# Second layer's gate and up products in five groups of seven block products, with the last product's operands split one product ahead and one weight sum made in DRAM

## The chip, the cores and the metric

The kernel runs on one core of a Trainium2 chip. The metric is the device time of one execution in microseconds (us). The engines are the matmul engine (PE, with its weight loads, PEld), VectorE (DVE), ScalarE (ACT), GpSimd (POOL) and SyncE (SP), which mainly issues DMAs.

## The reference

A decoder of two layers over x, 512 tokens by 1024 columns, in float32. Each layer has a mixer (the first a convolution beside differential attention, the second a gated delta rule beside forgetting attention) and then a gated product with D_FF = 2816:

```python
x = x + y @ w_out[l]
h = rms_norm(x, ffn_norm_w[l])
x = x + (jax.nn.silu(h @ w_gate[l]) * (h @ w_up[l])) @ w_down[l]
...
return rms_norm(x, final_norm_w)
```

What is changed is how `h @ w_gate[1]` and `h @ w_up[1]` are computed, and what `@ w_down[1]` needs for that. The mixers are not touched.

## The kernel before

Every operand of a large product is kept as a high part (rounded to the matmul engine's float32r by ACT) and a low part (what is left, by DVE), and a product is three matmuls: high by high, high by low, low by high (`product`, L2170, whose matmuls stand under L2168). "Split" below is that pair of an ACT copy and a DVE subtraction.

**Weights.** Weights come as tiles of 128 x 1024 floats, 512 KB, numbered t in the order of use. SP loads a tile into `raw` (two buffers), ACT and DVE split it into `wring`, a ring of RING = 4 slots, and PE uses it. `hi_ready`, `lo_ready` and `tile_used` are the counters between them: the split of tile t waits until tile t - 4 is used, the load of tile t into raw until the tile that was there is split. Each engine has its own program and does it in order; SP's and POOL's DMAs too go out in the order of their programs.

**First layer, gate and up.** Four plain tiles (`plain_gate_up`) of 8 x 3 = 24 matmuls of 512 columns each make the first two column chunks of gate and of up. The other 20 chunks of each come in GROUPED = 5 groups (`glu_products`, L2484). A group is a product of 512 rows by 1024 by 1024 columns, gate beside up, cut in 2 x 2 blocks and made with seven block products instead of eight: G_M11, G_M12, G_M22, G_M21, G_SUM, G_LAST, G_ALL, each two tiles of 12 matmuls, 14 steps in all. Here the activations are the stationary operand, so a group's result has tokens on the partitions; 16 transposes a group (`turn_results`, L2470, matmuls of L2481) turn it back, and stand in the next group ahead of its steps 4 and 6. The weights of the block products are sums. `x_part`, `y_part` and `w_part` are loaded by SP (`load_part`, L731), POOL's adding DMAs add a second block to x_part or w_part in place (L849), DVE adds y_part to x_part (`sum_weights`), and G_M12's tiles come through raw (L756). `x_part` has two buffers, x_even and x_odd, one for even and one for odd groups. `glu_hi` (L963, copies of L980) and `glu_lo` (L1498, L1504) split the tiles, `glu_results` (L1513) combines the block products on DVE, and `keep_turned` (L1010) copies turned chunks to their place `AF`.

**First layer, down** (`down`, L2503): the last group's transposes stand after the first eight chunk products and wait for DVE's last results.

**Second layer, gate and up** (`gate_up`, L2398): all 44 tiles plain, in a loop over four tiles; DVE evacuates them (L1464), ACT applies silu (L1065), and `ffn_last` on DVE (L1607) makes the chunks and the sums that the last product needs of them (`others`, `pfull`; L1622 to L1636). Before that loop DVE transposes x in blocks of 32 to `turned` (L2129), and SP moves those blocks to `resid`, x with tokens on partitions, with 16 DMAs of 128 KB in pieces of 128 bytes (`residual_blocks`, L774, L782), one after every second tile (RESIDUAL_AFTER, L66).

**Last product** (`w_down[1]`): again 2 x 2 blocks and seven products, of six pieces of up to 12 + 12 matmuls each (`piece`, L2808), in the order of L72: P_12, P_11, P_22, P_21, P_SUM, P_ALL, P_LAST. The blocks of w_down come from `last_d`: B12 through raw, B11 to `kept`, B22 to `more`, and POOL adds to both in place (`add_to_kept`, L896, L907); B11 + B21 + B22 is made by DVE's sums of kept and more (L1688). The left sides are split to their places (L1114, L1692) one product ahead from the third on, `last_lo` (L1643, L1648) splits the weights, and `after_product` (L1654) adds the products to resid.

**What sets the order around the change.** There is no planner here: each engine's program is written out by hand, with counters that say when a buffer is free. PE's order around the change is the second layer's output product (8 tiles), gate and up, the last product, and the end.

```python
            if t >= RESIDUAL_AFTER and (t - RESIDUAL_AFTER) % 2 == 0 and (t - RESIDUAL_AFTER) // 2 < 16:
                residual_blocks((t - RESIDUAL_AFTER) // 2)
...
                elif place is x_part[j % 2] and j >= 2:
                    t = glu_tile(j - 2, G_ALL, p)
                    sp.wait_ge(lo_ready[t % RING], slot_round(t))
```

## Time and profile before

| | |
|---|---|
| Time, median of 3 runs | 1218.61 us (1217.34 to 1218.65) |
| Time of the profiled execution | 1218.75 us |
| Its span, first to last instruction | 1216.9 us |
| PE matmuls busy | 1201.6 us, 99% |
| PE weight loads busy | 972.4 us, 80% |
| DVE busy | 784.4 us, 64% |
| ACT busy | 566.3 us, 47% |
| POOL busy | 107.1 us, 9% |
| Chain that ended last, share of PE | 89% |
| DMA | 138.04 MB, 113 GB/s over the span |

Times in the trace run from the span's start. The profiled execution took 1.85 us more than its span; that lies around the first and last instruction. The share of busy time is an average over stages with different limits, and a busy PE is one that has a matmul under way, not one at its peak: matmuls overlap, so the pace is read from how long many of them take together.

### The profile page before, as it was taken

Reading aid. Unit: us, or ns where it says so; the run is one execution under the profiler, and the core shown is the slowest. Engines: PE = TensorE matmul, PEld = TensorE weight load, DVE = VectorE, ACT = ScalarE, POOL = GpSimd, SP = SyncE. Lnnn points to the kernel's source line nnn. Section 1 sums busy time; section 2 is a strip of 40 time slices with the busy share of each in tenths; the row PEclk is TensorE's granted clock in tenths of the full one; section 3 lists DMA queues with packets and bytes.
Section 4 is the critical chain, followed back from the end, with each engine's and each line's share of the span. In section 5 each row is a group of like instructions: output and inputs, shape, how many; then the busy total and the mean of one; then the engine's idle time right before and its main releaser. Section 6 shows DMA issues by size and latency. Waiting matters only on the chain.

```text
span 1216.9 us, 16112 instructions
## 1 busy us (share of the span) xinstructions
PE 1201.6 (99%) x5831; PEld 972.4 (80%) x5831; DVE 784.4 (64%) x1233; ACT 566.3 (47%) x917; POOL 107.1 (9%) x209
## 2 busy tenths in 40 slices
PE   9999999999999999999999999999999999999998
PEld 7876648888888878888888788788888888888876
DVE  6787886786667763337677666545665455456796
ACT  6354455655555543325585254444243232324564
POOL 0000000011110100000002814400000000000120
PEclk9999999999999999999999999999999999999999
DMA  6243311687867533331322211022244443336881
GB/s 247 90 118 91 106 54 52 225 189 174 210 174 187 108 100 91 100 104 55 119 87 70 87 35 53 18 61 66 83 134 116 116 109 104 93 104 223 167 147 70
DMA packets 56643, 138.04 MB, mean 113 GB/s; under 512 B 21890, under 2 KB 22146, under 8 KB 56322
## 3 DMA queue, kind: packets, MB, share of 16 engines
q1 hardware_dynamic: 48754, 111.44, 28.7%
q0 software_dynamic: 6912, 24.38, 11.4%
q10 hardware_dynamic: 912, 1.35, 0.4%
q8 instruction: 40, 0.66, 0.2%
q14 instruction: 25, 0.20, 0.1%
HBM read 128.61 MB, written 2.10 MB: 107 GB/s over the span
## 4 chain that ended last, share of the span: by engine, by line
PE 89%; DVE 5%; ACT 3%; issue 1%; DMA 1%; ACTq 0%; SPq 0%; DVEq 0%
PE PS L2168 87%; PE PS L2481 1%; DVE wring L1648 1%; DMA raw<-w_stream 1%; PE PS L2244 1%; DVE resid L1652 0%; DVE kept L1688 0%; DVE cacc L1843 0%; ACT wring L924 0%; ACTq L1194 0%; DVE wring L1698 0%; PE PS L2559 0%; DVE AA L1692 0%; DVE out L2159 0%; DVE amax L1761 0%
## 5 line engine op out<-in xcount | busy, mean ns | idle before, releaser
L2168 PE MATMUL PS<-HH,wring 128*128 128x512 f32 x2136 | 506.2, 393 | 0.9 <-DVE vd L2094 0.9
L2168 PEld LDWEIGHTS PS<-HH,wring 128*128 128x128 f32 x2136 | 395.2, 188 | 81.4 <-issue 1.3
L2168 PE MATMUL PS<-wring,HH 128*128 128x512 f32 x672 | 156.0, 390 | 0.3 <-ACT wring L1139 0.3
L2168 PEld LDWEIGHTS PS<-wring,HH 128*128 128x128 f32 x672 | 125.7, 188 | 26.6 <-issue 0.6
L1698 DVE TENSOR_TENSOR wring<-raw,wring 128x1024 fp32r<-128x1024 f32 x91 | 111.8, 1231 | 48.2 <-ACT wring L924 48.1
L924 ACT ACTIVATE wring<-raw 128x1024 fp32r<-128x1024 f32 x91 | 95.8, 1056 | 96.0 <-PE PS L2168 68.6
L2168 PE MATMUL PS<-AS,wring 128*128 128x512 f32 x528 | 120.4, 389 | 0.0
L2168 PEld LDWEIGHTS PS<-AS,wring 128*128 128x128 f32 x528 | 99.0, 188 | 20.5
L2168 PE MATMUL PS<-wring,AA 128*128 128x512 f32 x462 | 105.4, 389 | 1.6 <-DVE wring L1648 0.8
L2168 PEld LDWEIGHTS PS<-wring,AA 128*128 128x128 f32 x462 | 86.6, 188 | 20.3 <-issue 2.3
L1464 DVE TENSOR_TENSOR ubuf<-PS,rstd 128x512 f32<-128x512 f32 x22 | 15.2, 690 | 83.9 <-PE PS L2168 83.9
L2168 PE MATMUL PS<-AA,wring 128*128 128x512 f32 x264 | 63.5, 394 | 0.4 <-DVE AA L1777 0.3
L2168 PEld LDWEIGHTS PS<-AA,wring 128*128 128x128 f32 x264 | 49.0, 188 | 11.7 <-issue 1.0
L952 ACT ACTIVATE wring<-raw 128x1024 fp32r<-128x1024 f32 x44 | 46.1, 1049 | 25.0 <-PE PS L2168 21.0
L1456 DVE TENSOR_TENSOR wring<-raw,wring 128x1024 fp32r<-128x1024 f32 x44 | 53.7, 1219 | 6.3 <-ACT wring L952 6.3
L2168 PE MATMUL PS<-wring,left_minus 128*128 128x512 f32 x240 | 56.8, 393 | 0.0
L1065 ACT ACTIVATE gbuf<-gbuf 128x512 f32<-128x512 f32 x22 | 13.9, 632 | 83.4 <-DVE gbuf L1464 83.4
L2168 PEld LDWEIGHTS PS<-wring,left_minus 128*128 128x128 f32 x240 | 44.5, 188 | 8.9
L1571 DVE TENSOR_TENSOR AS<-AF,AS 128x512 fp32r<-128x512 f32 x20 | 13.8, 689 | 47.6 <-ACT AS L1027 47.6
L907 POOL DMA_DIRECT2D kept<-w_last x12 | 10.4, 869 | 362.3 <-DVE wring L1648 344.3
L1504 DVE TENSOR_TENSOR wring<-x_even,wring 128x1024 fp32r<-128x1024 f32 x24 | 29.4, 1224 | 19.2 <-ACT wring L980 19.1
L849 POOL DMA_DIRECT2D x_even<-w_glu x12 | 10.5, 875 | 325.7 <-DVE wring L1504 325.7
(367 smaller groups left out, 1606.1 us busy)
## 6 DMA issues: line engine op xcount, KB each, us to landing
raw<-w_stream SPq DMA_DIRECT2D x131, 512.0 KB, 3.5
x_even<-w_glu POOLq DMA_DIRECT2D x12, 512.0 KB, 6.3
raw<-w_glu SPq DMA_DIRECT2D x10, 512.0 KB, 9.4
y_part<-w_glu SPq DMA_DIRECT2D x10, 512.0 KB, 6.6
w_part<-w_glu SPq DMA_DIRECT2D x10, 512.0 KB, 5.3
w_part<-w_glu POOLq DMA_DIRECT2D x10, 512.0 KB, 10.9
kept<-w_last POOLq DMA_DIRECT2D x10, 512.0 KB, 8.3
x_odd<-w_glu POOLq DMA_DIRECT2D x8, 512.0 KB, 6.2
```

The costliest lines, as they stand in the source:

```text
L924: nc.scalar.activation(wring[:, t % RING, 0], raw_tile(t), ACT.Copy).then_inc(hi_ready[t % RING], 1)
L952: nc.scalar.activation(wring[:, t % RING, 0], raw[:, t % RAW], ACT.Copy).then_inc(hi_ready[t % RING], 1)
L1065: nc.scalar.activation(gbuf[:, c], gbuf[:, c], ACT.Silu).then_inc(sem("gate_silu"), 1)
L1456: V.tensor_tensor(wring[:, t % RING, 1], raw[:, t % RAW], wring[:, t % RING, 0].bitcast(f32), ALU.subtract).then_inc(lo_ready[t % RING], 1)
L1464: V.tensor_tensor(buf[:, c], PS[:, 2 * c + u], rstd[:], ALU.mult).then_inc(evacuated, 1)
L1504: V.tensor_tensor(wring[:, t % RING, 1], glu_source(j, a, p), wring[:, t % RING, 0].bitcast(f32), ALU.subtract).then_inc(lo_ready[t % RING ...
L1571: V.tensor_tensor(AS[:, k % RING, 1], kept_chunk(k), AS[:, k % RING, 0].bitcast(f32), ALU.subtract).then_inc(sem("ffn_lo"), 1)
L1648: V.tensor_tensor(wring[:, t % RING, 1, 0:n], tile_source(g), wring[:, t % RING, 0, 0:n].bitcast(f32), ALU.subtract).then_inc(lo_ready[t % ...
L1698: V.tensor_tensor(wring[:, t % RING, 1], raw_tile(t), wring[:, t % RING, 0].bitcast(f32), ALU.subtract).then_inc(lo_ready[t % RING], 1)
L2168: return nc.tensor.matmul(out, lhsT, rhs, start=start, stop=stop, skip_group_check=adds)
L2244: last = nc.tensor.transpose(PS[:, bank, blk(j)], src[:, u % 2, blk(j)], ident)
L2481: last = nc.tensor.transpose(PS[:, TURN_BANK + c % 2, blk(b)], glu_result(b)[:, blk(c)], ident)
```

## The change

It does the following.

1. Second layer: four plain tiles, then five groups of seven block products as in the first layer, with the same functions, which now take the layer as their first argument. `gate_up` and DVE's and ACT's `ffn_last` go. After `load_group(1, 0)` SP issues the sixteen `residual_blocks`, all in a row, and then goes on with `load_group(1, 1)`. The blocks are transposed by DVE in steps 4 to 7 of the first group.
2. `x_part` has one buffer for all groups of both layers. It is loaded for group j + 1 as the last thing of `load_group(l, j)`, when G_ALL's tiles of group j are split.
3. First layer, down: half of the next two column products go ahead of each pair of transposes.
4. Last product: the order is P_12, P_11, P_21, P_22, P_SUM, P_LAST, P_ALL, four of the seven go on in a bank that holds an earlier one, the left sides lie in two places for even and odd products (`place_even`, `place_odd`) and are split one product ahead throughout, halves of columns are made during the groups (`halves`), cross sums in `cross`. The last group's transposes stand after three pieces of P_12.
5. B11 + B21 + B22 is made in DRAM (`w_sums`) by twelve DMAs of POOL, each waiting for the one before, that start when eight tiles have been used and stand ahead of the first layer's adding DMAs in POOL's program. SP loads it to kept for P_SUM. DVE's sums of kept and more go.

The core of the diff (the index functions with a layer argument, counters and the data layout of the host are left out):

```diff
-T_GLU = T_GU0 + 4
+PLAIN = 4
 GROUPED = 5
 GLU_PRODUCTS = 7
 GLU_STEPS = 2 * GLU_PRODUCTS
-T_DN0 = T_GLU + GROUPED * GLU_STEPS
+T_DN0 = T_GU0 + PLAIN + GROUPED * GLU_STEPS
 T_IN1 = T_DN0 + KF
 T_OUT1 = T_IN1 + 29
 T_GU1 = T_OUT1 + KD
-T_DN1 = T_GU1 + 2 * KF
+T_DN1 = T_GU1 + PLAIN + GROUPED * GLU_STEPS
+T_GLU = (T_GU0 + PLAIN, T_GU1 + PLAIN)
 AWAY = GROUPED * GLU_STEPS
-N_TILES = T_DN1 - AWAY
+N_TILES = T_GU1 + PLAIN - AWAY
 HALF = KF // 2
...
-P_12, P_11, P_22, P_21, P_SUM, P_ALL, P_LAST = range(PRODUCTS)
-OUT_ORDER = (2, 3, 0, 1)
-BANK_12, BANK_21, BANK_SUM, BANK_22 = 4, 6, 0, 2
-PRODUCT_BANK = (BANK_12, BANK_21, BANK_12, BANK_21, BANK_SUM, BANK_22, BANK_SUM)
+P_12, P_11, P_21, P_22, P_SUM, P_LAST, P_ALL = range(PRODUCTS)
...
+OUT_ORDER = (0, 1, 2, 3)
+PRODUCT_BANK = (4, 0, 4, 0, 2, 0, 4)
+CONTINUED = (P_21, P_22, P_LAST, P_ALL)
+ON_KEPT = (P_11, P_21, P_SUM, P_ALL)
 ADDED = (P_21, P_LAST, P_ALL)
 ADDING = 3
+SUM_PARTS, SUM_STEPS = 4, 3
...
+def uses_raw(t):
+    return not RAW <= t < FIRST and (not away(t) or (t - T_GLU[t >= T_GLU[1]]) % GLU_STEPS // 2 == G_M12) and t < T_DN1 + PIECES
...
-    AA, p = at("AA", [KF, 2, S], f32r, p)
-    gbuf, p = at("gbuf", [2, S], f32, p)
-    ubuf, p = at("ubuf", [2, S], f32, p)
+    AA, _ = at("AA", [KD, 2, S], f32r, p)
...
     AF, q = at("AF", [ENDING, S], f32, at_A)
-    AS, _ = at("AS", [RING, 2, S], f32r, q)
-    x_odd, q = at("x_odd", [2, TILE], f32, q)
+    at_left = q
+    AS, _ = at("AS", [RING, 2, S], f32r, at_left)
     left_diff, q = at("left_diff", [4, 2, 2 * P], f32r, q)
     left_minus, q = at("left_minus", [4, 2, S], f32r, q)
-    x_even, q = at("x_even", [2, TILE], f32, q)
+    at_parts = q
+    x_part, q = at("x_part", [2, TILE], f32, q)
...
     y_part, q = at("y_part", [2, TILE], f32, q)
     w_part, q = at("w_part", [2, TILE], f32, q)
+    pfull, q = at("pfull", [HALF, 2 * P], f32, q)
     assert q <= TOP, (q, TOP)
-    x_part = (x_even, x_odd)
     scaled, q = at("scaled", [KD, S], f32, at_A + 6 * S * 4)
+    turned, _ = at("turned", [NB, KD, P], f32, at_A + 6 * S * 4)
     diff_full, q = at("diff_full", [4, 2 * P], f32, q)
...
+    place_even, q = at("place_even", [HALF, 2, 2 * P], f32r, at_left)
+    assert q <= at_parts
+    place_odd, q = at("place_odd", [HALF, 2, 2 * P], f32r, at_parts)
+    assert q <= at_parts + 6 * TILE * 4
...
-        def load_part(place, sem_at, j, kh, u):
+        def load_part(l, place, sem_at, j, kh, u):
             for p in range(2):
                 n = sem_at + p
-                if place is w_part and j:
-                    t = glu_tile(j - 1, G_LAST, p)
+                if j:
+                    t = glu_tile(l, j - 1, G_LAST if place is w_part else G_M22 if place is y_part else G_ALL, p)
                     sp.wait_ge(lo_ready[t % RING], slot_round(t))
-                elif place is y_part and j:
-                    t = glu_tile(j - 1, G_M22, p)
-                    sp.wait_ge(lo_ready[t % RING], slot_round(t))
-                    sp.wait_ge(sem("lhs_made"), weights_summed(j - 1, p))
-                elif place is x_part[j % 2] and j >= 2:
-                    t = glu_tile(j - 2, G_ALL, p)
-                    sp.wait_ge(lo_ready[t % RING], slot_round(t))
-                sp.wait_ge(part_loaded[n], 16 * (j + 1))
-                sp.dma_start(place[:, p], glu_d[j, kh, u][:, p * TILE:(p + 1) * TILE]).then_inc(part_loaded[n], 16)
+                    if place is y_part:
+                        sp.wait_ge(sem("lhs_made"), weights_summed(l, j - 1, p))
+                sp.wait_ge(part_loaded[n], part_count(l, j) - 16)
+                sp.dma_start(place[:, p], glu_d[l, j, kh, u][:, p * TILE:(p + 1) * TILE]).then_inc(part_loaded[n], 16)
+        def load_group(l, j):
+            if j == 0:
+                load_part(l, x_part, 0, j, 0, 0)
+            for p in range(2):
+                t = glu_tile(l, j, G_M12, p)
+                before = raw_before(t)
+                sp.wait_ge(hi_ready[before % RING], slot_round(before))
+                sp.wait_ge(lo_ready[before % RING], slot_round(before))
+                sp.dma_start(raw[:, t % RAW], glu_d[l, j, 0, 1][:, p * TILE:(p + 1) * TILE]).then_inc(raw_loaded[t % RAW], 16)
+            load_part(l, y_part, 2, j, 1, 1)
+            load_part(l, w_part, 4, j, 1, 0)
+            if j + 1 < GROUPED:
+                load_part(l, x_part, 0, j + 1, 0, 0)
         sp.wait_ge(tile_used, T_OUT0 + RING)
         for j in range(GROUPED):
-            load_part(x_part[j % 2], 0, j, 0, 0)
-            for p in range(2):
-                t = glu_tile(j, G_M12, p)
-                before = t - GLU_STEPS if j else T_GLU - RAW + p
-                sp.wait_ge(hi_ready[before % RING], slot_round(before))
-                sp.wait_ge(lo_ready[before % RING], slot_round(before))
-                sp.dma_start(raw[:, p], glu_d[j, 0, 1][:, p * TILE:(p + 1) * TILE]).then_inc(raw_loaded[p], 16)
-            load_part(y_part, 2, j, 1, 1)
-            load_part(w_part, 4, j, 1, 0)
+            load_group(0, j)
...
                 sp.wait_ge(feed_sq, KD * FINAL)
+                sp.wait_ge(h_ready, KD * FINAL)
+                sp.wait_ge(sem("lhs_scaled"), 2 * KD)
...
-            if t == ROW_AFTER:
-                sp.wait_ge(ssq_done, 7 * FINAL)
-                sp.dma_start(final_w[:].rearrange("p a b -> p (a b)"), final_d).then_inc(small_loaded, 16)
-            if t >= RESIDUAL_AFTER and (t - RESIDUAL_AFTER) % 2 == 0 and (t - RESIDUAL_AFTER) // 2 < 16:
-                residual_blocks((t - RESIDUAL_AFTER) // 2)
+        sp.wait_ge(tile_used, T_GU1)
+        for j in range(GROUPED):
+            load_group(1, j)
+            if j == 0:
+                for m in range(16):
+                    residual_blocks(m)
         for i in range(PIECES):
             t = last_tile(i)
-            sp.wait_ge(hi_ready[(t - RAW) % RING], slot_round(t - RAW))
-            sp.wait_ge(lo_ready[(t - RAW) % RING], slot_round(t - RAW))
+            before = raw_before(t)
+            sp.wait_ge(hi_ready[before % RING], slot_round(before))
+            sp.wait_ge(lo_ready[before % RING], slot_round(before))
             n = len(piece_rows(i)) * S
             sp.dma_start(raw[:, t % RAW, 0:n], last_d[B12][:, columns_of(i)]).then_inc(raw_loaded[t % RAW], 16)
         sp.wait_ge(tile_used, T_DN1)
         for i in range(PIECES):
+            sp.wait_ge(kept_loaded[i], kept_count(P_11) - 16)
             sp.dma_start(kept_tile(i), last_d[B11][:, columns_of(i)]).then_inc(kept_loaded[i], 16)
+        sp.dma_start(more_last[:], last_d[B22][:, 3 * TILE:HALF * S]).then_inc(first_loaded[1], 16)
+        sp.wait_ge(sem("glu_turned"), 8 * GROUPED)
         sp.dma_start(more_first[:], last_d[B22][:, 0:3 * TILE]).then_inc(first_loaded[0], 16)
-        sp.wait_ge(sem("ffn_lo"), SPLITS_0 + HALF)
-        sp.wait_ge(sem("lhs_made"), MADE)
-        sp.dma_start(more_last[:], last_d[B22][:, 3 * TILE:HALF * S]).then_inc(first_loaded[1], 16)
+        sp.wait_ge(sem("ffn_lo"), split_count(P_11, PIECES - 1))
+        sp.wait_ge(sem("halves_made"), 2 * HALF)
+        sp.dma_start(final_w, final_d.rearrange("p (u c) -> p u c", u=2)).then_inc(small_loaded, 16)
+        sp.wait_ge(added[0], GROWN_FIRST)
+        for i in range(PIECES):
+            t = last_tile(P_21 * PIECES + i)
+            sp.wait_ge(lo_ready[t % RING], slot_round(t))
+            sp.dma_start(kept_tile(i), sums_d[:, columns_of(i)]).then_inc(kept_loaded[i], 16)
...
+        quarter = HALF * S // SUM_PARTS
+        pool.wait_ge(tile_used, T_IN0 + 8)
+        for step in range(SUM_STEPS):
+            for n in range(SUM_PARTS):
+                columns = slice(n * quarter, (n + 1) * quarter)
+                if step or n:
+                    pool.wait_ge(added[0], 16 * (SUM_PARTS * step + n))
+                if step:
+                    nc.gpsimd.dma_start(sums_d[:, columns], last_d[(B11, B21, B22)[step]][:, columns], accum_op=ALU.add).then_inc(added[0], 16)
+                else:
+                    nc.gpsimd.dma_start(sums_d[:, columns], last_d[B11][:, columns]).then_inc(added[0], 16)
...
+        def grow_group(l, j):
...
+                                accum_op=ALU.add).then_inc(added[d % ADDING], 16)
+        for a, part, behind in ((P_21, B21, P_11), (P_LAST, B21, P_22), (P_ALL, B12, P_SUM)):
             for i in range(PIECES):
-                add_to_kept(a, i, part, behind)
...
+                if g == 4:
+                    keep_turned(1, GROUPED - 1, 0)
+                    left_high(P_12, 4)
+                    keep_turned(1, GROUPED - 1, 2)
+                    left_high(P_12, 5)
+                    keep_turned(1, GROUPED - 1, 1)
+                    keep_turned(1, GROUPED - 1, 3)
                 if g == 9:
...
+        def halves(r):
+            if r == 0:
+                dve.wait_ge(sem("ffn_mul"), MULS + 2)
+            else:
+                dve.wait_ge(sem("glu_kept"), 4 * GROUPED + (2 * r if r < HALF - 2 else 4 * GROUPED - HALF + 1 + r))
+            first, second = kept_chunk(2 * r), kept_chunk(2 * r + 1)
+            V.tensor_tensor(first[:, 2 * P:S], first[:, 2 * P:S], second[:, 2 * P:S], ALU.subtract).then_inc(sem("halves_made"), 1)
+            dve.wait_ge(sem("halves_made"), 2 * r + 1)
+            V.tensor_tensor(pfull[:, r], first[:, 0:2 * P], first[:, 2 * P:S], ALU.subtract).then_inc(sem("halves_made"), 1)
+        def turn_residual(n):
+            if n == 0:
+                dve.wait_ge(sem("ffn_lo"), SPLITS[1] + 1)
+                dve.wait_ge(sem("ffn_hi"), SPLITS[1] + 1)
+                dve.wait_ge(sem("lhs_made"), SUMS + LEFT_SUMS)
+            V.transpose(turned[:, :, n], xT[:, n].rearrange("p (t c) -> p t c", c=P)).then_inc(sem("resid_turned"), 1)
...
+            elif l and 4 <= step < 8:
+                for n in (2 * step - 8, 2 * step - 7):
+                    turn_residual(n)
...
+        def cross(a, i):
+            dve.wait_ge(sem("halves_made"), 2 * HALF)
+            of = P_22 if a == P_LAST else P_21
+            dve.wait_ge(sem("ffn_lo"), split_count(of, i))
+            start, stop = rows_of(i)
+            V.tensor_tensor(full_left(a, i), full_left(a, i), pfull[:, start:stop], ALU.subtract).then_inc(sem("halves_made"), 1)
...
-                if g // PIECES == P_21:
-                    i = g % PIECES
-                    dve.wait_ge(first_loaded[i // 3], 32)
-                    dve.wait_ge(lo_ready[last_tile(g) % RING], slot_round(last_tile(g)))
-                    V.tensor_tensor(kept_tile(i), kept_tile(i), more_tile(i), ALU.add).then_inc(sem("lhs_made"), 1)
...
+            pe.wait_ge(sem("copied"), COPIED)
+            columns(4, range(RING))
+            pe.wait_ge(sem("ffn_mul"), glu_made(0, end, "gate_first", 1))
+            columns(0, (0, 1))
+            turn_results(0, end, (0, 1), TURN_BANK)
+            columns(0, (2, 3))
+            pe.wait_ge(sem("ffn_mul"), glu_made(0, end, "up_second", 1))
+            columns(2, (0, 1))
+            turn_results(0, end, (2, 3), TURN_BANK)
+            columns(2, (2, 3))
+            pe.wait_ge(sem("glu_kept"), COPIED)
...
-        gate_up(T_GU1, E_GU1, 3)
+        plain_gate_up(1, T_GU1, E_GU1)
+        for j in range(GROUPED):
+            glu_products(1, j)
...
+                if a == P_12 and i == 3:
+                    pe.wait_ge(sem("ffn_mul"), glu_made(1, GROUPED - 1, "up_second", 1))
+                    turn_results(1, GROUPED - 1, (0, 2, 1, 3), LAST_TURN_BANK)
```

## Rows read from the trace of the kernel before

**Rows 1.** The page, busy time of each engine with its share of the span

```profile
PE 1201.6 (99%) x5831; PEld 972.4 (80%) x5831; DVE 784.4 (64%) x1233; ACT 566.3 (47%) x917; POOL 107.1 (9%) x209
```

**Rows 2.** The chain that ended last, in the first layer's groups: start, length, what

```profile
296.42 0.87 PE PS L2481 x8
...
303.64 32.66 PE PS L2168 x144
336.30 0.87 PE PS L2481 x8
...
416.10 0.87 PE PS L2481 x8
```

**Rows 3.** Windows: a first-layer group, then plain second-layer tiles (busy us and count by engine)

```profile
325.00:365.00 40.00, 40.00 (x186) 33.26 (x185) 28.06 (x31) 21.27 (x27) 5.21 (x6) 1.00 0.75 185
...
925.00:968.00 43.00, 43.00 (x192) 35.59 (x191) 21.48 (x30) 14.18 (x16) 0.00 (x0) 1.00 0.39 106
```

**Rows 4.** DVE: transposes for resid; subtractions of half rows, with busy time and mean ns

```profile
L2129 DVE STREAM_TRANSPOSE turned<-xT x8: 668/669/711, 876.6 to 880.8; 128x512 f32<-128x512 f32 x8
...
L1622 DVE TENSOR_TENSOR others<-ubuf 128x256 f32 x11 | 4.6, 418 | 0.0
```

**Rows 5.** Timeline at the seam of two groups of the first layer: start, length, engine

```profile
314.25 3.05 SPq L746 DMA_DIRECT2D x_odd<-w_glu  x2
...
315.72 1.23 DVE L1504 TENSOR_TENSOR wring<-x_odd,wring 128x1024 fp32r<-128x1024 f32 x1 [1.49 <-ACT wring L980]
...
318.44 1.23 DVE L1504 TENSOR_TENSOR wring<-x_even,wring 128x1024 fp32r<-128x1024 f32 x1 [1.49 <-ACT wring L980]
319.96 0.86 POOL L849 DMA_DIRECT2D x_even<-w_glu  x1 [12.86 <-DVE wring L1504]
...
325.18 3.05 SPq L756 DMA_DIRECT2D raw<-w_glu  x2
```

**Rows 6.** DMA issues: count, KB each, median us from issue to landing

```profile
raw<-w_stream SPq DMA_DIRECT2D x131, 512.0 KB, 3.5
...
raw<-w_glu SPq DMA_DIRECT2D x10, 512.0 KB, 9.4
...
kept<-w_last POOLq DMA_DIRECT2D x10, 512.0 KB, 8.3
```

**Rows 7.** The resid copies; SP's DMA queue in 905.7 to 906.1 and in 905.2 to 906.3

```profile
L782 SPq DMA_DIRECT2D resid<-turned x16: 597/597/687, 886.9 to 1044.7; - x16
...
DMA to landing us min/median/max: 3.9/4.7/6.1
...
q1 hardware_dynamic: 529, 0.07, 106.7%
...
q1 hardware_dynamic: 1069, 0.18, 89.0%
```

**Rows 8.** Windows: where the granted clock (the third last number) falls

```profile
780.00:784.00 4.00, 3.15 (x27) 2.13 (x26) 3.00 (x8) 2.32 (x6) 0.00 (x0) 1.00 0.00 0
784.00:788.00 4.00, 4.00 (x24) 4.00 (x23) 1.05 (x3) 0.87 (x2) 0.00 (x0) 0.57 0.00 0
```

**Rows 9.** First layer's end: a window, and PE's first transposes after the last group

```profile
440.00:460.00 20.00, 18.50 (x90) 15.25 (x89) 8.72 (x11) 6.19 (x9) 0.00 (x0) 1.00 0.33 106
...
452.05 0.41 PE L2481 MATMUL PS<-consts,hbuf 128*128 128x128 f32 x2 [1.50 <-DVE glu_s L1542]
```

**Rows 10.** Last product: DVE's weight sums, and the window in which they stand

```profile
L1688 DVE TENSOR_TENSOR kept<-kept,more_first 128x1024 f32<-128x1024 f32 x3 | 3.7, 1226 | 0.3
...
1142.00:1166.00 24.00, 22.45 (x98) 17.97 (x98) 21.83 (x27) 13.87 (x21) 5.16 (x6) 1.00 0.67 110
```

**Rows 11.** Eighth tile's result on DVE; POOL's first adding DMA; landings of w_part's DMAs

```profile
56.34 0.69 DVE L1827 TENSOR_TENSOR ub<-hbuf,sqb 128x512 f32<-128x512 f32 x1 [2.41 <-ACT sqb L1185]
...
241.69 1.01 POOL L849 DMA_DIRECT2D x_even<-w_glu  x1 [240.23 <-DVE wring L1504]
...
DMA to landing us min/median/max: 4.2/9.6/12.2
```

More of the change, by code:

```diff
@@ L2126, in _ @@
         out_proj(3, T_OUT1, E_OUT1)
[L2127 to L2130 removed]
+        ffn_gated(1, T_GU1, E_GU1)
         last_product()
@@ L2910 @@
     out = nc.dram_tensor("out_t", (NB, P, D), f32, kind="ExternalOutput").ap()
-    build(nc, *args, out)
+    sums = nc.dram_tensor("w_sums", (P, HALF * S), f32, kind="Internal").ap()
+    build(nc, sums, *args, out)
     r = run_bass_kernel_spmd(nc, [arrays], core_ids=[0])
```

798 lines of the change are left out of this document (392 added, 406 removed).

## The prediction

> **What bounds the kernel now.** The page comes first: the matmul engine (PE) is busy 1201.6 of 1216.9 us, so only PE's own work, or a wait long enough to stop PE, can move the end [rows 1]. VectorE (DVE), ScalarE (ACT) and the DMA matter by what they make PE wait for. The chain of waits shows what a grouped stage costs: in the first layer the transposes of the groups recur at 296.42, 336.30 and 416.10, so a group lasts 39.88 us, and 144 products take 32.66 us, 0.2268 us each [rows 2]. The windows show both stages packed: the plain second layer has PE busy 43.00 of 43.00 us with DVE at 21.48, a group has PE 40.00 of 40.00 with DVE at 28.06 and ACT at 21.27 [rows 3]. PE has no holes in either, so what a hole costs is new time.
>
> **Second layer's gate and up.** Removed: 40 of 44 plain tiles, each 24 products: 960 x 0.2268 = 217.7 us. Added: five groups of 14 tiles of 12 products, 840 x 0.2268, and 80 transposes, of which the trace has eight in 0.87 us. That is five times the measured group, 5 x 39.88 = 199.4 us [rows 2]. **Saved: 18.3 us.** DVE and ACT work stays covered: on a group's 28.06 us DVE gets four subtractions of half rows (0.42 us each) and in the first group eight transposes of 0.67 us [rows 3, 4]; the first group has no results of a group before it to finish. If that cover were gone each microsecond would count, but 12 us per group are free.
>
> **One x_part instead of two.** Both layers now load the next group's first tiles only once the last sum of this group has been split. In a group that begins at 325.4 (its first transposes, at 336.30, come 48 products later) those splits were DVE's at 313.00 and 315.72, and SP issued the reload of that same buffer at 314.25 and 317; the next group's first split was at 318.44 [rows 2, 5]. Such a load lands in about 4.5 us, so the first split moves to about 321, still 4 us ahead of PE. Loads of raw, y and w follow in one burst of some 3.5 MB; even the slow landing of 9.4 us [rows 6] brings raw at 327, and it is needed split at 330.8. I cost this at nothing; what hides it is the ring of four tiles, and the margin is 2 to 4 us a group, which is the first thing to go if DMA is slower (eight seams, at most 3 us each, 24 us).
>
> **Residual moves past SP's queue.** This is the costly part. Before, one of the sixteen small-block copies into resid was issued every second tile. Now all sixteen stand in SP's program after the load of group 1's x_part and before the load of its raw tiles, which PE needs 5.44 us into the group. With G the start of that group: the last x_part load can go at G - 8.4 (316.95 against 325.4) [rows 5], the sixteen issue for 0.60 us each, 9.6 us, and raw is issued at G + 1.5. They share its DMA queue. One copy's 1024 pieces filled 1.1 us at 89% of all DMA engines, and in its dense middle 529 pieces passed in 0.4 us, so a copy costs the engines between 0.8 (0.4 x 1024 / 529) and 1.1 us [rows 7]. I take 0.85, near the dense middle, since copies in a row overlap their ragged ends: 13.6 us. The first block moves about 2 us after its issue (landing 3.9 at the least, less 1.1 of data and a receipt), at G - 6, so they end at G + 7.6. The two adding DMAs of x_part, issued by POOL at G - 4.4 and G - 1.7, take part of the engines: I add 2 us of a possible 5. Raw's own 512 KB take 1.4 us and a receipt of 0.4, so it lands at G + 11.4; high and low split (1.06 and 1.23 us) put it at G + 13.8. PE stands from G + 5.4: 8.4 us. **The stop cannot be made up**, as PE is the bound. After it the results and splits that queued on DVE and ACT come out one by one before the first transposes; I take 1.6 us. **Together +10 us.** Bounds: if only issue counts, raw lands 3.5 us after G + 1.5 [rows 6] and the cost is 2 us; at 1.1 us a copy, with all 5 us of the adding DMAs and 3 us of catching up, it is 17 us; if copies in a row cost 2 us each, near half their 4.7 us landing, 29 us.
>
> **The clock.** The granted clock falls once in this trace: it is 0.57 in 784 to 788, after PE was busy only 3.15 of the 4 us before [rows 8]. That is a stretch at the lower level (1.2 GHz instead of 2.4) and is worth at most 4 x 0.43 = 1.7 us of PE. A stop of 8 us should bring the same; I let it coincide with the catching up above, whose work needs that time anyway, and keep 1.7 us for the upper end. The Trainium skill (TensorE: Matmul & The Clock Gate, "Why this matters for your kernels") warns that an idle gap between bursts of matmuls sends the clock back to half; by that rule alone I would add the 1.7 us and get 1211.
>
> **First layer's end.** PE stands 1.50 us in 440 to 460, since the transposes at 452.05 wait for DVE's glu_s [rows 9]. The change puts 12 more products (2.7 us) ahead of them: **-1.5 us**.
>
> **Into the last product.** The last group's transposes now stand after three pieces (36 products, 8.2 us) of the last product, against the 7.3 us from start to transpose seen in the first layer: no stop. But pieces 4 and 5 need their left sides from those columns: copies, splits, halves of the columns and two low splits follow in a row, some 4 us after the first transposes end, while PE has one piece, 2.7 us: **+1.3 us** (0 to 3). The other left sides are split one product ahead.
>
> **Last product's weights.** DVE's sums kept + more (1.23 us each, five and a half of them) go [rows 10]; where they stood PE was busy 22.45 of 24 us: **-1.0 us** of the 1.55, as cross sums of 0.7 us come in nearby. P_21 now has one product less of lead for its adding DMAs; issued about 15 us before PE's need, with a landing of 8.3 us [rows 6], they stay hidden.
>
> **Weight sum in DRAM.** Twelve DMAs of 720 KB, each waiting for the one before, from about 56 us (the eighth tile's result) [rows 11]. They stand on POOL's queue ahead of the first adding DMA of the first layer, issued at 241.69. So each may take (241.7 - 56.3) / 12 = 15.4 us. The nearest row, the loads and adding DMAs of w_part of 512 KB each, has landings of 4.2 to 12.2 us under load [rows 11], by size 6 to 17 us; alone, as here, I take 7 to 9: done by 165. Other loads there have slack of several tiles: 0 (to +3 for the copies of the convolution's inputs). The Trainium skill (DMA: Bandwidth & Descriptors, "Anatomy of one DMA") fits 2.0 us plus size at 436 GB/s, an estimate of 3.7 us each and 44 us in all, which does not change the sum; it also calls a write to HBM the slowest to confirm, and no row here shows one of that kind.
>
> **Sum**, against the profiled execution (1218.75 us, its span plus 1.85; 0.14 above the median of 1218.61, which is nothing): 1218.75 - 18.3 - 1.5 + 1.3 - 1.0 + 10.0 = **1209.3 us**.
>
> **Rivals.** (1) The copies hardly delay raw (only the issue counts, or raw overtakes them): 10 becomes 0 to 4, so 1199 to 1203. For it: pieces of 128 bytes pass quickly in the dense middle [rows 7]; against it: nothing follows them closely in this trace, and SP's 9.6 us alone are past the margin. (2) **Slower:** the copies in a row cost the queue 2 us or more each. 16 x 2 ends at G + 26, raw is ready at G + 32, and the stop is 27 us with 2 of catching up: 1228. It decides from a stop of about 22 us, 1.6 us a copy. For it: a single copy takes 4.7 us to land, and a raw load with adding DMAs beside it 9.4 against 3.5 [rows 6, 7]; against it, the 1.1 us of engine time. (3) The DRAM chain is slower than 15.4 us a step: at 18 us it ends 31 us late, of which the first group hides 9: about 1231. No row for such a DMA exists; I hold it for unlikely, at twice the row nearest to it. (4) The single x_part leaves a stop of 1 to 3 us at the seven other seams too: 1216 to 1230 with the copies.
>
> **Chances.** Forecast (stop of 5 to 17 us, 1204 to 1216): 0.55. Rival 1: 0.22. Rival 2: 0.10. Rival 3: 0.04. Rival 4: 0.09, half of it slower. Range 1198 to 1222: it leaves out the far half of rival 2, rival 3 and the ends. A measurement of this kernel tells 0.2%, 2.4 us, from no change: faster (below 1216.2) 0.81, same 0.06, slower 0.13.
>
> **What would show it.** Five groups near 39.9 us in both layers, except the second layer's second, near 49; there the first raw split waits for a DMA from w_glu, with sixteen resid issues in one row of SP before it; PE idle near 8 us, the granted clock perhaps low after it; PE full in 445 to 460; about 1 us idle before the fifth piece of the last product. Wrong if PE is full at that seam, if POOL's first x_part addition comes after 242 us, or if groups of the first layer exceed 40 us.

## The result, and the profile after

The changed kernel takes 1221.16 us (median of 12 runs, 1219.51 to 1224.3) against 1217.74 of the kernel before (12 runs): ratio 1.0027, 95% interval 1.0019 to 1.0034. It is slower by 0.27%, where 1209.3 us, faster, was forecast. The profiled execution is 1221.2 us with a span of 1219.4.

The page of after, against [rows 1]: the busy time of each engine, two rows of the slices (the span in 40 equal parts), and the chain that ended last.

```profile
PE 1186.4 (97%) x5791; PEld 959.2 (79%) x5791; DVE 837.8 (69%) x1273; ACT 619.4 (51%) x992; POOL 141.9 (12%) x251
...
PE   9999999999999999999999999999995899999998
...
PEclk9999999999999999999999999999998899999999
...
PE 85%; DVE 6%; ACT 3%; SPq 2%; issue 2%; DMA 2%; ACTq 0%; DVEq 0%
PE PS L2263 82%; SPq L817 2%; PE PS L2559 1%; DMA first_raw<-w_stream 1%; DVE wring L1571 1%; PE PS L2339 1%; DVE cacc L1939 0%; DMA x_part<-w_glu 0%; ACTq L1275 0%; DVE wring L1794 0%; DMA raw<-w_glu 0%; ACT wring L1036 0%; ACT wring L984 0%; DVE turned L1630 0%; DVE amax L1857 0%
```

PE does 15.2 us less work, and the span is 2.5 us longer: PE now stands for 33 us instead of 15. Two slices of the PE row show it (5 and 8), a dip of PEclk lies over them, and the chain has a link that no page of before had: SPq L817, SP issuing the residual copies. The waits of PE name the stops (us in total, times, longest):

```profile
PE PS L2263 <- DVE glu_s L1603: 17.3, 1, 17.3
PE PS L2263 <- DVE glu_q L1589: 1.6, 1, 1.6
...
PE PS L2263 <- DVE place_even L1674: 1.2, 1, 1.2
```

The large one is one stop, in the second layer's second group. The timelines of SP, ACT, DVE and PE there (start, length, engine, line):

```profile
915.21 2.78 SPq L772 DMA_DIRECT2D x_part<-w_glu  x2
918.16 20.49 SPq L817 DMA_DIRECT2D resid<-turned  x16
938.74 1.11 SPq L783 DMA_DIRECT2D raw<-w_glu  x2
...
943.44 1.06 ACT L1036 ACTIVATE wring<-raw 128x1024 fp32r<-128x1024 f32 x1 [19.87 <-DMA raw<-w_glu]
...
944.52 1.23 DVE L1571 TENSOR_TENSOR wring<-raw,wring 128x1024 fp32r<-128x1024 f32 x1 [18.50 <-ACT wring L1036]
946.70 1.23 DVE L1571 TENSOR_TENSOR wring<-raw,wring 128x1024 fp32r<-128x1024 f32 x1 [0.94 <-ACT wring L1036]
947.84 1.28 DVE L1603 TENSOR_TENSOR glu_s<-PS,glu_s 128x512 f32<-128x512 f32 x2
...
926.08 5.78 PE L2263 MATMUL PS<-wring,left_diff 128*128 128x512 f32 x24
949.18 7.77 PE L2263 MATMUL PS<-wring,HH 128*128 128x512 f32 x24 [17.32 <-DVE glu_s L1603]
```

Followed backwards: PE waits for glu_s, which empties a bank; on DVE glu_s stands behind both low splits of raw; ACT's high split waited 19.87 us for raw to land; and SP issued raw only at 938.74, after sixteen copies that took 20.49 us to issue, 1.28 us each. Raw lands at 943.4, 17.4 us into the group; 11.4 was forecast. The releaser that the wait names is the last link, not the cause. The order on DVE has a part in it all the same: the first raw tile was split at 945.75, but PE ran only at 949.18, since glu_s (L1603) stands behind the second split, although its input, the last product of the group before, had been there since about 926. That is at most 3.4 us of the 17.3, an estimate from these rows; no run moved L1603.

The 24 products after the stop take 7.77 us; in the kernel of 1198.7 us below, where PE had waited 0.32 us before them, the same 24 take 5.74 us. Windows of after (busy us and count by engine, granted clock, DMA share, GB/s):

```profile
936.00:940.00 4.00, 0.00 (x0) 0.00 (x0) 0.00 (x0) 0.00 (x0) 0.00 (x0) 0.56 1.07 178
...
948.00:952.00 4.00, 2.82 (x7) 2.25 (x8) 4.00 (x6) 0.56 (x1) 1.72 (x2) 0.50 0.48 139
952.00:956.00 4.00, 4.00 (x16) 3.22 (x15) 2.63 (x4) 2.15 (x3) 0.00 (x0) 0.80 1.04 193
```

The granted clock falls to its lower level (1.2 GHz instead of 2.4) while PE stands, and is still there when PE starts again: 2.0 us more. In the other runs below with a stop of 6.9 us or more at this place the 24 products take 7.51 to 8.48 us, so 1.8 to 2.7 us more.

### The profile page after: what moved, and what is told of

The parts are those of the page before. It is cut to its first block, busy times and chain, and to the rows that moved or that the text cites. A ratio compares the mean times of both kernels' runs of the same rounds, so it can differ in the third digit from the quotient of the medians.

```text
span 1219.4 us, 15948 instructions
## 1 busy us (share of the span) xinstructions
PE 1186.4 (97%) x5791; PEld 959.2 (79%) x5791; DVE 837.8 (69%) x1273; ACT 619.4 (51%) x992; POOL 141.9 (12%) x251
## 4 chain that ended last, share of the span: by engine, by line
PE 85%; DVE 6%; ACT 3%; SPq 2%; issue 2%; DMA 2%; ACTq 0%; DVEq 0%
PE PS L2263 82%; SPq L817 2%; PE PS L2559 1%; DMA first_raw<-w_stream 1%; DVE wring L1571 1%; PE PS L2339 1%; DVE cacc L1939 0%; DMA x_part<-w_glu 0%; ACTq L1275 0%; DVE wring L1794 0%; DMA raw<-w_glu 0%; ACT wring L1036 0%; ACT wring L984 0%; DVE turned L1630 0%; DVE amax L1857 0%
## 5 line engine op out<-in xcount | busy, mean ns | idle before, releaser
L2263 PE MATMUL PS<-HH,wring 128*128 128x512 f32 x1176 | 288.7, 397 | 0.9 <-DVE vd L2191 0.9
L2263 PE MATMUL PS<-wring,HH 128*128 128x512 f32 x1152 | 268.7, 392 | 17.6 <-DVE glu_s L1603 17.3
L2263 PEld LDWEIGHTS PS<-wring,HH 128*128 128x128 f32 x1152 | 217.2, 189 | 63.4 <-DVE glu_s L1603 17.7
L2263 PEld LDWEIGHTS PS<-HH,wring 128*128 128x128 f32 x1176 | 215.0, 188 | 44.0 <-issue 1.3
L1571 DVE TENSOR_TENSOR wring<-x_part,wring 128x1024 fp32r<-128x1024 f32 x80 | 97.9, 1224 | 77.3 <-ACT wring L1036 77.2
L1794 DVE TENSOR_TENSOR wring<-raw,wring 128x1024 fp32r<-128x1024 f32 x91 | 111.9, 1232 | 46.2 <-ACT wring L984 46.2
L1036 ACT ACTIVATE wring<-x_part 128x1024 fp32r<-128x1024 f32 x80 | 84.6, 1060 | 107.1 <-PE PS L2263 45.9
L2263 PE MATMUL PS<-wring,left_minus 128*128 128x512 f32 x480 | 113.8, 393 | 1.6 <-DVE glu_q L1589 1.6
L2263 PEld LDWEIGHTS PS<-AS,wring 128*128 128x128 f32 x528 | 99.0, 188 | 20.5
L2263 PE MATMUL PS<-wring,place_even 128*128 128x512 f32 x264 | 61.1, 390 | 1.2 <-DVE place_even L1674 1.2
L2263 PE MATMUL PS<-wring,left_diff 128*128 128x512 f32 x240 | 56.5, 391 | 0.4 <-DVE hbuf L1600 0.4
```

The source lines that it names most:

```text
L1036: nc.scalar.activation(wring[:, t % RING, 0], glu_source(t, a, p), ACT.Copy).then_inc(hi_ready[t % RING], 1)
L1571: V.tensor_tensor(wring[:, t % RING, 1], glu_source(t, a, p), wring[:, t % RING, 0].bitcast(f32), ALU.subtract).then_inc(lo_ready[t % RING ...
L1794: V.tensor_tensor(wring[:, t % RING, 1], raw_tile(t), wring[:, t % RING, 0].bitcast(f32), ALU.subtract).then_inc(lo_ready[t % RING], 1)
L2263: return nc.tensor.matmul(out, lhsT, rhs, start=start, stop=stop, skip_group_check=adds)
```

## The experiments

Ratios are against runs of the kernel before on the same chip, whose medians were 1217.6 to 1217.7 us; after itself was not run again there. A seam is the change from one group to the next. The recorded expectations count the kernels: the first is the one with the copies behind the loads, the fourth adds the spread transposes to it, the fifth adds the copies in two parts to the fourth, the ninth is the one of 1198.7 us. An edit shifts the line numbers behind it by one to three, so go by the names of the tiles.

**The copies behind the loads.** The copies leave their place ahead of raw and stand behind the w load of the same group.

```
             load_part(l, w_part, 4, j, 1, 0)
+            if l and j == 1:
+                for m in range(0, 16):
+                    residual_blocks(m)
...
-            if j == 0:
-                for m in range(16):
-                    residual_blocks(m)
```

> The kernel after, with one move in SP's program: the sixteen residual copies stand behind the raw, y and w loads of the second layer's second group instead of ahead of them. Nothing is left out. Theory (the copies hold up the raw loads behind them in SP's queue, and this alone made the kernel slower): the PE stop of 17.3 us at 931.9 goes, and so does the half clock behind it, worth 2.3 us: 1221.2 - 19.6 = 1201.6 us, 1200 to 1204. Rival A (the stop is the seam's own: one x_part buffer, y and w loads in one burst, DVE behind): the stop stays or moves to another load, 1215 to 1221. Rival B (the copies take the DMA engines from whatever comes next, the additions to x_part and w_part or the next x_part load): a new stop of 3 to 8 us in that group, 1205 to 1210.

Measured: 1204.1 us (1202.8 to 1205.9), ratio 0.989 (0.988 to 0.991), 17.1 us less than after. The stop at the second product is gone and the clock stays at 1.00. Timeline of SP and of PE at the next seam, 40 us on:

```profile
922.08 35.56 SPq L820 DMA_DIRECT2D resid<-turned  x16
957.73 1.11 SPq L772 DMA_DIRECT2D x_part<-w_glu  x2
...
967.31 5.73 PE L2263 MATMUL PS<-wring,left_diff 128*128 128x512 f32 x24 [2.13 <-DVE hbuf L1600]
```

The theory holds, 2.5 us short of its figure. Rival B's stop in that group did not come, a smaller one did at the next seam: the copies, now behind the y and w loads and beside six of POOL's additions, take 35.56 us of SP, the next x_part load goes late, and PE stands 2.1 us there.

**How the stop grows.** The same move with eight, and with four, of the copies left ahead of raw (`range(8)` or `range(4)` ahead, the rest behind w).

> The kernel after, with eight of the sixteen residual copies ahead of the raw loads as now and the other eight behind the w load. Nothing is left out. It gives the slope of the stop per copy. In the trace of after SP took 20.5 us for sixteen (1.28 us each); in 935 to 940, where the copies had the DMA engines to themselves, 7092 packets of them passed, 0.72 us for a copy's 1024. Theory: the copies cost engine time, and the additions to x_part share it; raw lands 8 x 1.28 = 10 us earlier and the stop is about 7 us: 1211 us, 1208 to 1213. Rival 1 (0.72 us a copy, the rest is the additions and stays): stop of 11.5 us, 1215. Rival 2 (the price is a step, not a slope: a queue that fills up after the first few): either no stop at all, 1202, or nearly all of it, 1219.

> The kernel after, with four of the sixteen residual copies ahead of the raw loads and twelve behind the w load. Nothing is left out. With 16, 8 and 0 ahead PE stood 17.3, 9.6 and 0 us. Theory (a slope of 0.96 us per copy beyond what the margin hides): stop of 5 to 6 us; 1204.1 + 5.5 = 1209.6 us, or 1212 if so short a stop also brings the half clock of 2.3 us that both longer ones brought. Rival (the first copies pass before the additions begin and inside the margin): stop of 0 to 3 us, 1204 to 1207, the clock unbroken.

Measured: 1213.5 us with eight (8 runs; ratio 0.996, 0.995 to 0.997), 1211.6 with four (2 runs; 0.995, 0.993 to 0.997). SP and PE with eight, then with four:

```profile
916.81 13.87 SPq L820 DMA_DIRECT2D resid<-turned  x8
...
940.79 7.88 PE L2266 MATMUL PS<-wring,HH 128*128 128x512 f32 x24 [9.63 <-DVE glu_s L1606]
```

```profile
916.58 4.97 SPq L820 DMA_DIRECT2D resid<-turned  x4
...
937.29 7.80 PE L2266 MATMUL PS<-wring,HH 128*128 128x512 f32 x24 [6.88 <-DVE glu_s L1606]
```

With 0, 4, 8 and 16 copies ahead PE stands 0, 6.9, 9.6 and 17.3 us: 1.7 us a copy for the first four, 0.7 for the next four, 1.0 for the last eight. It is no step, but no straight line either: with eight copies the stop lies between the theory's 7 us and rival 1's 11.5, and the time is above the theory's range; with four both stop and time are near what was expected. The 7.80 us behind a stop of 6.9 us show that this stop brought the lower clock too (with four copies the time is 7.5 us above the kernel with none ahead); stops of up to 2.3 us at the seams left it at 1.00.

**What made a copy dear.** First the same bytes in long rows; then the small pieces with POOL's two additions held back.

```
-            sp.dma_start(to[:, :, a], from_[:, :, b]).then_inc(sem("resid_loaded"), 16)
+            to = resid.rearrange("p t u c -> p (t u c)")[32 * b:32 * b + 32, 1024 * a:1024 * (a + 1)]
+            from_ = turned.rearrange("p t n c -> p (t n c)")[32 * a:32 * a + 32, 1024 * b:1024 * (b + 1)]
+            sp.dma_start(to, from_).then_inc(sem("resid_loaded"), 16)
```

> The kernel after, with sixteen copies of the same 128 KB at the same place in SP's program, but each moves 32 rows of 4 KB instead of 1024 pieces of 128 bytes, so the residual is not turned and the output is another one. Theory (engine time of the small pieces): the copies need no more than 0.3 to 0.4 us of the engines each, SP issues all in about 10 us, raw is issued at 928 and lands at 931.5 to 934, the stop is 2 to 5 us: 1203 to 1207. Rival (the number of DMAs in a row is what counts, 1.28 us each whatever they move): stop as in after, 1220 to 1222.

```
+                if l and j == 1 and n == 0:
+                    pool.wait_ge(sem("resid_loaded"), 16 * 16)
```

> The kernel after, with the two additions to x_part of the second layer's second group held back until all residual copies have landed. Nothing is left out. In 920 to 935 of after these additions had 63, 35 and 22% of the DMA engines beside the copies. Theory (they made a copy cost 1.28 us instead of 0.72): the copies are through in 12 to 13 us, at about 933 instead of 940, raw lands at 936 to 937 instead of 943.4, and the stop shrinks by 6 to 7 us: 1214 to 1216, unless the additions, now landing at about 941 to 945, are late in turn for their product. Rival 1 (the additions cost the copies nothing, SP or one engine's order sets the pace): 1221. Rival 2 (the additions become the new wait): stop of 5 us and another of up to 8, 1219 to 1222.

Measured: long rows 1215.7 us with 15.1 us of SP and a stop of 11.4; additions held back 1213.3 us with 13.7 us of SP and a stop of 10.8. SP and PE with the additions held back:

```profile
915.86 13.68 SPq L817 DMA_DIRECT2D resid<-turned  x16
...
940.31 7.51 PE L2265 MATMUL PS<-wring,HH 128*128 128x512 f32 x24 [10.79 <-DVE glu_s L1605]
```

The DMA queues of after in 935 to 940, where the copies are alone, and of after and of the long rows in 920 to 930, where the additions run too (packets, MB, share of 16 engines, which can read a little over 100%; q1 is SP's queue, q0 POOL's):

```profile
q1 hardware_dynamic: 7092, 0.90, 107.2%
...
DMA packets 5487, 1.78 MB, mean 178 GB/s; under 512 B 5212, under 2 KB 5212, under 8 KB 5487
...
q1 hardware_dynamic: 5267, 0.94, 51.1%
q0 software_dynamic: 220, 0.84, 49.0%
```

```profile
q1 hardware_dynamic: 440, 1.20, 52.0%
q0 software_dynamic: 239, 0.91, 50.4%
```

Alone, a copy's 1024 pieces take 5 x 1.072 x 1024 / 7092 = 0.77 us of the engines: the forecast's 0.85 was near. What was wrong is the company. Over these 10 us, while the additions last, the two queues get about half of the engines each, and 5212 pieces, 5.1 copies, go through: 2.0 us a copy instead of 0.77 (the last of the x_part load is in SP's half too). Held back, the additions give back 6.8 us of SP and 6.5 us of the stop, within the theory's 6 to 7; the time of 1213.3 is 0.7 us below its range. The long rows fail both expectations, of a stop of 2 to 5 us and of one as in after: 128 KB in rows of 4 KB still took some 0.57 us of the engines (52.0% of 10 us for 1.20 MB), not 0.3, and shared them like the others. So the small pieces are only 5.4 us of SP's 20.5 and 5.9 of the stop; the additions are worth a little more. The two were not taken away together, so how they add up is not shown.

**The pairs of transposes.** One turned copy in each of the steps 4 to 11, on top of the first experiment's kernel.

```
-            elif l and 4 <= step < 8:
-                for n in (2 * step - 8, 2 * step - 7):
-                    turn_residual(n)
+            elif l and 4 <= step < 12:
+                turn_residual(step - 4)
```

> The first experiment's kernel (all copies behind the second group's w load), and the eight turned copies of the residual on VectorE made one each in steps 4 to 11 of the second layer's first group instead of two each in steps 4 to 7. Nothing is left out. Theory (those pairs, 1.30 us each, are why glu_q came late and PE stood 1.60 us at 903): the 1.60 us go, 1204.1 - 1.6 = 1202.5 us. Rival (the wait is the queue of the left-side splits ahead of them, 3.5 us in a row, and stays): 1204.1, and the idle before glu_q's waiter is still 1.6.

Measured: 1205.0 us (1203.8 to 1211.5). The 1.6 us of idle are gone, and nothing is gained between the medians: the idle behind hbuf L1600 went from 3.2 to 5.1 us, 1.71 of it at the very next seam, near 926. That is no accident of one execution: with the transposes spread and L1600 late, PE stood 1.4 to 2.3 us at that seam in all three profiles, with them in pairs 0 to 1.4 us in six. But 2.4 of the 5.1 us stand in the first layer (1.05 before), which this edit does not touch; that much is scatter.

**The copies in two parts.** Twelve behind the second group's w load, four behind the third's.

> As the kernel with the turned copies spread, and the residual copies in two parts: twelve behind the second group's w load, four behind the third group's. Nothing is left out. In the first experiment SP issued its sixteen from 922.1 to 957.7, beside four additions of POOL, so the third group's x_part load went out about 3 us late and PE stood 2.1 us for a split at that seam. Theory (a load held up again by copies ahead of it): twelve are through by 949, the 2.1 us go, and the time is 1202.5 - 2.1 = 1200.4 us, 1199.5 to 1201.5. Rival (the 2.1 us belong to the seam with its one x_part buffer): 1202.5, the idle at that seam unchanged.

Measured: 1206.9 us (1203.8 to 1210.9), no gain; the two ranges overlap. The stop aimed at, at the third group's seam, is gone. ACT and PE in the third group:

```profile
960.86 16.48 SPq L820 DMA_DIRECT2D resid<-turned  x4
...
983.62 1.09 ACT L1043 ACTIVATE AF<-PS 128x512 f32<-128x512 f32 x2 [5.96 <-DMA resid<-turned]
984.36 0.41 PE L2558 MATMUL PS<-consts,hbuf 128*128 128x128 f32 x2 [1.50 <-ACT AF L1043]
```

The four late copies took 16.48 us behind y, w and the additions, and ACT may not overwrite `turned` before they land: a new wait of 1.5 us, and the other seams still cost 4.6, 1.62 of it at the next one.

**The weight sum in DRAM.** The kernel with the copies in two parts, its eight adding DMAs cut to 64 columns.

> The fifth experiment's kernel with the eight adding DMAs of the weight sum in DRAM cut to 64 columns each (some 32 KB instead of 704 KB); the four plain copies stay whole. The sum is so left out for most columns and the output is another one. Theory (the chain ends long before the first layer's groups and costs nothing): the same time as the fifth kernel within 1 us, about 1200.4. Rival (its 17 MB of traffic delay the input loads or the weights of the stages up to 150 us): 1 to 4 us less, 1197 to 1199.

Measured: 1206.8 against 1206.9 us. In 60 to 150 the DMA moved 134 GB/s instead of 195, and PE was busy 90.00 of 90 us in both. The first group begins at 247.30 us with the chain whole and at 247.47 with it cut (247.19 in after, 247.29 in before, which has no chain). The chain costs nothing.

**The order of results and splits at a seam.** The seams' stops all waited for L1600, so this changes the order alone. The three kernels are the ninth, the same with the transposes in pairs, and after with nothing but the early result.

```
-                if step == 1:
+                if step == 0:
                     glu_results(l, j - 1, "gate_first")
```

> The fourth experiment's kernel (all copies behind the w load, turned copies spread) with one more move on VectorE: the gate_first results of a group (L1600), which free the bank that the next group's first product writes, come ahead of the next group's second x_part split instead of behind it. Nothing is left out. In the fourth kernel PE stood 5.1 us in five pieces for L1600, which followed the split of an x_part tile that had just landed. Theory (the seams stop PE because gate_first is queued behind a split whose load comes late; PE needs the split itself only 2.7 us or more later): these 5.1 us go, 1205 - 5 = 1200 us, 1198 to 1201.5, and the runs lie closer together than 1203.8 to 1211.5. Rival (the load is so late that PE waits for the split itself): the waits change their name to the x_part splits and 2 us or less are saved, 1203 to 1205.

> The same as the kernel with gate_first early, but the turned copies in pairs in steps 4 to 7 as in after. Nothing is left out. With the seams quiet it isolates the pairs. Theory: 1.6 us more than the kernel with them spread, about 1201.5, idle of 1.6 us before the product that follows glu_q. Rival (a gain here is given back at the next seam, as it was between the first and the fourth experiment, where 1.6 us less idle at 903 left the time the same): no difference within 0.5 us.

> The kernel after with gate_first ahead of the second x_part split and nothing else: the copies stay ahead of the raw loads. Nothing is left out. Theory (the seams cost after only the 0.4 us seen at 325, the copies' stop is a raw load's and not gate_first's): 1220.5 us, 1219.5 to 1221.2. Rival (the late gate_first adds to the stop of 17.3 us, since results queue behind late splits): 1217 to 1219.

Measured: with the copies behind the loads and the transposes spread, **1198.7 us** (1198.5 to 1199.7), ratio 0.984 (0.983 to 0.986), faster than before and after; with the transposes in pairs 1200.1 (1199.6 to 1203.1); with the early result alone, the copies still ahead of raw, 1218.2 (11 runs, 1216.6 to 1219.0; ratio 1.000, 0.999 to 1.001), 3.0 us less than after. The last is below the theory's range and in the rival's, though not by its mechanism: the stop did not change. DVE at one first-layer seam, in after and with the early result alone:

```profile
323.38 1.23 DVE L1571 TENSOR_TENSOR wring<-x_part,wring 128x1024 fp32r<-128x1024 f32 x1 [2.45 <-ACT wring L1036]
324.52 1.28 DVE L1600 TENSOR_TENSOR hbuf<-PS,glu_s 128x512 f32<-128x512 f32 x2
```

```profile
320.21 1.28 DVE L1600 TENSOR_TENSOR hbuf<-PS,glu_s 128x512 f32<-128x512 f32 x2
322.98 1.23 DVE L1571 TENSOR_TENSOR wring<-x_part,wring 128x1024 fp32r<-128x1024 f32 x1 [1.49 <-ACT wring L1036]
```

PE's product at 325.5 needs the bank that L1600 empties. Behind the split of a tile that has just landed, L1600 comes 0.4 us too late; ahead of it, 3.5 us early (done at 321.5, needed at 325.0). Now that the seams are quiet (1.6 us in two pieces are left, 1.3 of them where the copies delay an x_part load) the pairs' 1.6 us show as 1.4 between the medians. In the kernel with the early result alone the first layer's groups all come at 39.9 us, and the stop of 17.1 us is unchanged. Of its 3.0 us the two profiled executions show 1.0 by the end of the first layer, 0.65 of it at the seam; another 1.7 lie between there and 904, where only after's profile has the clock at its lower level, near 783 (as before had, [rows 8]), and that is hardly the edit's. How much of the 3.0 between the medians is the seams' stays open.

**The copies in another queue.** POOL issues them, behind its additions to x_part and ahead of those to w_part; the rest as in the 1198.7 us kernel.

```
+            nc.gpsimd.dma_start(to[:, :, a], from_[:, :, b]).then_inc(sem("resid_loaded"), 16)
...
+                if l and j == 1 and n == 2:
+                    for m in range(16):
+                        residual_blocks(m)
```

> The ninth experiment's kernel (gate_first early, turned copies spread), but the sixteen residual copies are issued by POOL behind its two additions to x_part, so from about G + 1 on, at the same stretch as in after but in another queue than the raw, y and w loads. Nothing is left out. Theory (what stopped PE was the place of the copies ahead of raw in one queue, not that they run then): raw is issued at G - 10 and lands before the copies begin, no stop at G + 5.4, and with SP free the third group's x_part load is on time, so the 1.3 us seen there go too: 1197 to 1199 us. Rival (copies running beside the weights stop PE whoever issues them; or POOL needs over 2 us for each, so that its additions to w_part come more than 10 us late): a stop of 5 to 25 us in that group, 1203 to 1222.

Measured: 1218.0 us (10 runs; ratio 1.000, 0.999 to 1.001). POOL and PE:

```profile
933.87 2.44 POOL L885 DMA_DIRECT2D resid<-turned  x3 [8.15 <-DMA w_part<-w_glu]
...
961.74 1.88 POOL L907 DMA_DIRECT2D w_part<-w_glu  x2
...
970.73 12.60 PE L2262 MATMUL PS<-wring,HH 128*128 128x512 f32 x48 [17.59 <-DVE wring L1571]
```

The rival holds, by its second half: POOL took 1.7 us a copy, and its additions to w_part went out at 961.74, against 931.02 in the ninth kernel. The theory was right only where it looked: there is no stop at the second product, where raw was free, but one of 17.6 us where the additions to w_part were queued behind the copies. Both say the same, that what stands behind the copies in their own queue comes late. POOL issued three, paused 2.5 to 4.5 us, and issued three more: 28 us for sixteen. The insertion also stood behind a wait for w's landing, and began 8 us later than meant; without that the stop should be shorter, which was not tried.

## Why the prediction was wrong

**Second layer's gate and up: right.** Its groups' transposes recur at 956.95, 996.85, 1036.75 and 1076.65, 39.90 us each, against 39.88 forecast:

```profile
996.85 0.87 PE PS L2559 x8
...
1036.75 0.87 PE PS L2559 x8
```

By this pace the 18.3 us were gained.

**The residual copies: the step that failed,** in size and not in mechanism. The forecast had a stop of 8.4 us, 1.6 of catching up, and the clock at nothing. Measured: 17.3 and 2.0, 19.3 instead of 10. The term "I add 2 us of a possible 5" for the adding DMAs was mis-sized: held back, they proved to be worth 6.5 us of the stop. The 0.85 us a copy was near (0.77), and the first block's start too (16 small packets before 920, 2525 in 920 to 925). Raw landed 6.0 us later than forecast: about 4.5 because the copies ended near 940, 14 us into the group instead of 9.6, the rest behind them, where raw took some 3 us instead of 1.8 (no row shows the receipt of 0.4 us in that sum). After raw's landing it took 5.7 us until PE ran, 4.0 in the forecast, since glu_s stood behind both low splits; and PE stopped 0.4 us later than forecast. That is 6.0 + 1.7 - 0.4 = 7.3, and the clock makes it 9.3.

The upper bound of 17 us was added up wrong: by its own terms it is 8.4 + 4 (1.1 us a copy) + 3 (the adding DMAs) + 3 (catching up) = 18.4, and the 19.3 lie above that too. The time is inside the stated range of 1198 to 1222, at its slow end, but it moved the other way than forecast; slower had a chance of 0.13. That the range holds it is luck in part, since it was not made of the losses that came. Rival 2 had the right direction, from the wrong price (2 us or more of the queue a copy; 1.28 measured, under its threshold of 1.6), because the clock and the smaller losses below joined it.

**The clock: wrong to cost it at nothing.** I let it coincide with the catching up; but PE's own work ran at half speed after it. The rule that I had quoted from the Trainium skill (TensorE: Matmul & The Clock Gate, "Why this matters for your kernels"), that an idle gap sends the clock back to half, agrees with the rows of the long stop: 0.50 in 940 to 952. The short stops at the seams, up to 2.3 us, left it at 1.00. The price was 2.0 us, where I had bounded it by 1.7.

**The turned copies on DVE: wrong.** "12 us per group are free" is an average over a group. In 886 to 904 DVE had four pairs of 1.30 us between splits of 1.2, glu_q came late and PE stood 1.6 us. Spreading them took the stop away.

**One x_part: wrong in what it watches.** The margin of 2 to 4 us was worked out to PE's need of the split tile. The first thing that PE needs there is L1600 behind it, and that margin was about nothing: a wait of 0.4 us in the profile of after, up to 6.6 in the profiles of its variants. Rival 4 was a part of the truth.

**First layer's end: right. Last product: right in the stop, low in the gain.** PE is busy 15.00 of 15 us in 445 to 460 (-1.5). The stop into the last product is 1.23 us (+1.3 forecast). In 1120 to 1205 PE is busy 85.00 us against 83.44 before, 1.6 us for a forecast of 1.0. **Weight sum in DRAM: right,** nothing, by the experiment; a DMA landed in 6.7 us at the median (7 to 9 forecast), and the last was issued at 129.3.

Sum, from profile to profile: -18.3 + 17.3 + 2.0 + 1.6 + 0.65 (the seam at 325, with what its group lost) - 1.5 + 1.2 - 1.6 = +1.4; measured 1221.2 - 1218.75 = +2.5. About 0.9 of the 1.1 us between lies in the second layer's first two groups: from first product to first product they take 40.13 and 59.72 us, where 38.1 (the ninth kernel's first group) and 39.9 with the stops and the clock named give 39.7 and 59.2. What it is stays open. With the copies' term at zero the forecast's own sum is 1199.3, and the kernel without the stop, the late result and the pairs takes 1198.7. That they agree to 0.6 us is partly luck: that kernel still stands 1.6 us at seams, and the last product gave 0.6 us more than forecast.

## What to carry to other kernels

A transfer moved within a queue costs what is behind it: look at what is issued next in the same queue and when it is needed, and add the other queues' transfers of that stretch in full; here POOL's had about half of the engines for as long as they lasted (49% and 50% over 10 us). At the place where a late tile meets an engine's program, ask which instruction stands behind its split, not only when the split itself is needed. Put results that free a bank ahead of splits of tiles that are still to land; here one number in one `if` was worth 6 us between the medians, once the large stop was gone, and at most 3 us while it was there.

## What was not expected of the hardware

Sixteen copies of 128 KB in a row held their issuing queue for 20.5 us (1.28 us each) though alone each takes 0.60 [rows 7]; with long rows 0.95, with no additions beside them 0.86, behind y and w loads with six additions 2.2, and issued by POOL 1.7, in threes with pauses of 2.5 to 4.5 us. It looks as if the issuing engine is held back by the transfers ahead; what holds it was not measured by itself. And removing a stop in one place widened the next: in the profiles 1.6 us less at 903 came back as 1.7 at 926, until the order of two DVE instructions was changed.
